# Experts' down products last, in two passes, with half of the second block's projections under the second pass

## The chip, the core and the metric

The kernel runs on one core of one Trainium2 chip. The metric is device microseconds of one execution, the median of several runs. All data are float32.

## What is computed

Two transformer blocks on x (256 tokens, 1024 features). The first ends in an expert-choice FFN with 16 experts of 32 tokens each and a hidden width of 2048; its result is normed. The second block projects its own norm of that by w_in_2 (7168 columns: q, k, v, z, two gates), adds a context, mixes, and ends in PEER, whose rows are gathered from a table. Cut to what matters here:

```python
hid = silu(einsum('becd,edf->becf', xs, w_gate)) * einsum('becd,edf->becf', xs, w_up)
eo = einsum('becf,efd->becd', hid, w_down)
x = x + zeros.at[bidx, idx].add(gates[..., None] * eo)       # first block, FFN
x = rms_norm(x, final_g)
h = modulate(rmsnorm(x, g_pre_mix), sh1, sc1)                # second block
q, k, v, z, gl = split_proj(h @ w_in_2)
y = mix_branches(rope(q), [kc, rope(k)], [vc, v], z, gl + b_gate, ...)
x_new = x + gt1 * rmsnorm(y, g_post_mix)
x = x_new + gt2 * rmsnorm(peer(modulate(rmsnorm(x_new, g_pre_ffn), sh2, sc2)), g_post_ffn)
```

## The kernel before, in words

Each engine has a program of its own, written as one Python function (`tensor`, `vector`, and so on); events are semaphore counts. A wait names an event, such as ("used", key) for "PE has finished with this weight block". PE is the matmul engine, DVE the vector engine, ACT the scalar engine, POOL the one that gathers, SP the one that issues the weight transfers. SP is one queue in program order: `load(slot, key, src)` waits for the last user of the slot in SBUF, then issues the transfer; `ring` takes the next slot of a list. A block is 2 MB (128 x 4096 floats).

Experts: for e in 0..15, `gate` and `upw` (four blocks each, L704) use 32 columns of the PE array per matmul, four column groups side by side; HID is transposed (L717); `down` (four blocks, L728) gives all 1024 features of the expert's 32 tokens in bank BE; DVE copies them (L1253), and four full-width matmuls (L742) with a gate matrix GE spread them over the tokens in banks YB. After expert 15, `block_out` and `gained` add and scale (L1266, L1270), `both_norms` and `norm_turn` make HT, the second block's input, features on partitions.

Second block: `mixer_order` returns ORDER, a list of stages that all engines walk. q, k and v (L800, `seven`) are made with seven instead of eight block products each, with DVE sums of weights (`wsum`) and inputs (`hsum`). `z`, `ga`, `gs` go through `tokens` (L416), eight matmuls of 128x512 each, one per half of the features and half of the tokens. They stand as fillers between the stages of the attention heads: `sc` scores (L837), `exp`, `cmb`, `trn` transpose (L846), `av` values (L858), `ao`. After the heads of token half a = 0 come `ba`, `op`, the norms and `ft`, then `qm` (L904), the first query product of PEER, then the gathers (`row`, L1994), which run to the end; the other half of the tokens is worked off beside them.

Of the kernel before, what the change touches and what calls it, by code (L numbers as in the profile page):

```python
# [14 lines left out]
NS = 6  # L15
SLOT = 4096
NARENA = 25832
# [104 lines left out]
def build(nc, D, out):  # L122
    from contextlib import ExitStack
    ctx = ExitStack()
    with ctx:
# [42 lines left out]
        LSUM, SSO, sub8, ssy, ss5, ss6, s8 = small(32), small(16), small(8), small(4), small(2), small(2), small(4)  # L168
        lamc = lam[:, 2:3]
# [14 lines left out]
        LATER, GE, OH, EO = ar(o, 8, 384), ar(o + 3072, 2, 2, 256), ar(o + 4096, 2, 512), ar(o + 5120, 2, 512)  # L184
# [4 lines left out]
        HDT = ar(o + 7168, 4, 128)  # L189
# [12 lines left out]
        YB, BG, BU, BH, BE = [0, 1, 2, 3], 4, 5, 6, 7  # L202

# [5 lines left out]
        RAW, RT, TMPG = ar(o + 14336, 2, 512), ar(o + 15360, 2, 512), ar(o + 14336, 2, 1024)  # L209
        PP, TT, AA, ATT = ar(o + 16384, 2, 2, 512), ar(o + 18432, 512), ar(o + 18944, 2, 512), ar(o + 19968, 2, 512)  # L210
        HSUM = ar(2048, 4, 4, 128)
        WSUM = {(m, i): ar(k, 4, 512) for m, at in (("k", (o + 8192, o + 12288, o + 6144)), ("q", (o + 16384, o + 18432, o + 10240)),
                                                    ("v", (o + 8192, o + 12288, o + 6144))) for i, k in zip((5, 6, 4), at)}
        DM, OYT = ar(o + 20992, 16, 8), HT
# [18 lines left out]
        def joined(m, a, n):  # L233
            d = QX[:, a, :, :].rearrange("p h t -> p (h t)") if m == "q" else VX[:, a, :]
            return d[:, n * 512:(n + 1) * 512]


        BLOCK = {"q": 0, "k": 2, "v": 4}
        RESULT = {1: (0, 0), 2: (0, 0), 6: (0, 1), 3: (0, 1), 4: (1, 0), 7: (1, 1)}
        place = [NARENA + i * SLOT for i in range(NS)] + [W0, SPARE, o + 21120, o + 14336, o, o + 16384, *PLACES]  # L240
# [7 lines left out]
        def mixer_order():  # L248
# [4 lines left out]
            def do(text):  # L253
                for word in text.split():
# [3 lines left out]
            do("norm_turn.0 seven.k.1 norm_turn.1 seven.k.2 hsum.0 wsum.k.5 hsum.1 wsum.k.6 seven.q.1 hsum.2 wsum.k.7 hsum.3 wsum.k.4 x3")  # L258
            do("seven.q.2 seven.k.5 seven.k.6 join.k.2 turned.k.0.0 join.q.2 wsum.q.5 wsum.q.6 seven.k.7 join.k.7 rope.k.0.0 seven.q.5 seven.k.4")
            do("turned.k.1.1 wsum.q.7 wsum.q.4 seven.k.3 join.k.3 turned.k.0.1 turned.k.1.0 seven.q.6 rope.k.1.1 seven.q.7 join.q.7")  # L260
            do("turned.q.0.0 turned.q.1.1 rope.k.0.1 seven.v.1 rope.k.1.0 seven.q.4 wsum.v.5 wsum.v.6 seven.q.3 join.q.3 turned.q.0.1")
            do("wsum.v.7 wsum.v.4 turned.q.1.0 seven.v.5 rope.q.0.0 rope.q.1.1 seven.v.6 seven.v.2 join.v.2 rope.q.0.1 seven.v.7 join.v.7")
            do("rope.q.1.0 seven.v.4 seven.v.3 join.v.3")
# [1988 lines left out]
```

## Time and profile before

| | |
|---|---|
| runs | 2100.95, 2101.39, 2102.20 us (median 2101.39) |
| profiled execution, span | 2100.0 us (what lies around it is not given; the median run is 1.4 us longer) |
| PE / DVE / ACT / POOL busy | 71% / 37% / 21% / 14% |
| bytes moved | 807.99 MB, mean 385 GB/s |
| chain that ended last | DMA 49%, PE 35%, DVE 9% |

The span is from the first to the last instruction of one execution. Busy shares are means over stages that differ; the stages have to be looked at one by one. In the profile each float32 matmul shows as two instructions, so a count such as x16 is eight matmuls of the program.

### The profile page before, as it was taken

How to read it: one execution, taken by the hardware profiler on the slowest of the kernel's cores; microseconds unless marked ns; L12 is line 12 of the kernel's file. 1: busy time of each engine (PE TensorE's matmuls, PEld its weight loads, DVE VectorE, ACT ScalarE, POOL GpSimd, SP SyncE). 2: the span in 40 equal slices, each digit the busy share in tenths (PEclk: the TensorE clock that was granted, in tenths of full speed). 3: DMA queues.
4: the chain of work that ended last, by engine and by line, in shares of the span. 5: the costliest groups of instructions: out<-in, count | busy, mean ns of one | idle time of the engine just before them, and what ended most of it. 6: DMA issues, size and time to landing. Idle time of an engine off the chain costs nothing.

```text
span 2100.0 us, 24929 instructions
## 1 busy us (share of the span) xinstructions
PE 1498.3 (71%) x10450; PEld 641.7 (31%) x10450; DVE 775.6 (37%) x1885; ACT 437.2 (21%) x990; POOL 302.6 (14%) x289
## 2 busy tenths in 40 slices
PE   9999756877676666566889999996667744444344
PEld 7654212332111111111344455553235510000001
DVE  5832101000000000000007443347667676867764
ACT  1331100000000000000002274453245622211212
POOL 0010000000000000000000000004334344544441
PEclk9999888898888778888999999997788865655555
DMA  9799999999999999999994556579999999999997
GB/s 401 288 402 424 427 427 428 427 428 428 428 427 428 428 428 427 428 428 428 427 410 191 211 196 240 209 290 387 405 422 418 420 421 420 421 421 420 421 421 293
DMA packets 76176, 807.99 MB, mean 385 GB/s; under 512 B 9024, under 2 KB 9152, under 8 KB 10400
## 3 DMA queue, kind: packets, MB, share of 16 engines
q1 hardware_dynamic: 38432, 537.74, 61.3%
q0 software_dynamic: 37632, 268.65, 30.9%
q8 instruction: 83, 1.36, 0.3%
q14 instruction: 29, 0.24, 0.0%
HBM read 805.11 MB, written 1.05 MB: 384 GB/s over the span
## 4 chain that ended last, share of the span: by engine, by line
DMA 49%; PE 35%; DVE 9%; ACT 3%; issue 2%; POOL 2%; DVEq 0%; ACTq 0%; POOLq 0%
DMA AR<-in_w_down 19%; DMA AR<-in_w_up 16%; DMA AR<-in_peer_uv,AR 15%; PE PS L416 11%; PE PS L427 4%; PE PS L800 3%; DVE AR L1580 3%; PE PS L704 3%; PE PS L728 2%; POOL AR L1994 2%; PE PS L947 2%; PE PS L537 1%; PE PS L904 1%; PE PS L742 1%; PE PS L494 1%
## 5 line engine op out<-in xcount | busy, mean ns | idle before, releaser
L1994 POOL DMA_INDIRECT AR<-in_peer_uv,AR x256 | 287.0, 1121 | 1611.9 <-DVE AR L1571 1307.2
L947 PE MATMUL PS<-AR 32*32 32x512 f32 x4032 | 219.6, 909 | 293.3 <-ACT AR L1932 293.2
L704 PE MATMUL PS<-AR 128*32 128x512 f32 x2048 | 297.9, 718 | 159.4 <-DMA AR<-in_w_up 111.6
L1580 DVE CUSTOM_DVE_ANT_0 AR<-AR 128x1024 f32<-128x1024 f32 x256 | 309.4, 1223 | 161.1 <-DMA AR<-in_peer_uv,AR 160.8
L416 PE MATMUL PS<-AR 128*128 128x512 f32 x544 | 243.3, 602 | 0.0
L728 PE MATMUL PS<-AR 128*32 128x512 f32 x1024 | 164.1, 775 | 88.4 <-DMA AR<-in_w_down 80.0
L1238 DVE TENSOR_TENSOR AR<-AR,PS 128x512 f32<-128x512 f32 x16 | 11.0, 688 | 581.3 <-PE PS L704 581.3
L704 PEld LDWEIGHTS PS<-AR 128*32 128x32 f32 x2048 | 62.2, 121 | 377.8 <-DMA AR<-in_w_up 179.3
L947 PEld LDWEIGHTS PS<-AR 32*32 32x32 f32 x4032 | 36.8, 125 | 431.9 <-ACT AR L1932 426.2
L416 PEld LDWEIGHTS PS<-AR 128*128 128x128 f32 x544 | 102.8, 193 | 127.1 <-issue 126.4
L1253 DVE COPY AR<-PS 128x512 f32<-128x512 f32 x16 | 11.1, 692 | 275.1 <-PE PS L728 275.1
L1926 ACT ACTIVATE AR<-AR 128x2 f32<-128x2 f32 x126 | 25.6, 203 | 380.0 <-DVE AR L1580 379.7
L1757 ACT ACTIVATE AR<-PS 128x512 f32<-128x512 f32 x16 | 9.6, 597 | 411.4 <-PE PS L704 411.4
L728 PEld LDWEIGHTS PS<-AR 128*32 128x32 f32 x1024 | 33.0, 127 | 199.1 <-DMA AR<-in_w_down 126.1
L427 PE MATMUL PS<-AR 128*128 128x256 f32 x384 | 84.2, 380 | 0.5 <-DVE AR L1013 0.5
L742 PE MATMUL PS<-AR 128*128 128x512 f32 x128 | 66.7, 669 | 14.5 <-DVE AR L1253 14.5
L427 PEld LDWEIGHTS PS<-AR 128*128 128x128 f32 x384 | 72.6, 190 | 14.0 <-issue 3.5
L800 PE MATMUL PS<-AR 128*128 128x512 f32 x168 | 74.3, 595 | 2.0 <-ACT AR L1821 1.2
L904 PE MATMUL PS<-AR 128*128 128x128 f32 x512 | 70.2, 302 | 7.1 <-DVE AR L1503 3.9
L904 PEld LDWEIGHTS PS<-AR 128*128 128x128 f32 x512 | 67.5, 216 | 13.2 <-issue 6.6
L1932 ACT ACTIVATE AR<-AR 128x32 f32<-128x32 f32 x252 | 67.3, 314 | 8.9
L437 PE MATMUL PS<-PK 128*128 128x256 f32 x248 | 62.8, 402 | 3.1 <-DMA PK<-in_pk 3.1
(297 smaller groups left out, 1389.9 us busy)
## 6 DMA issues: line engine op xcount, KB each, us to landing
AR<-in_w_up SPq DMA_DIRECT2D x64, 2048.0 KB, 25.7
AR<-in_w_down SPq DMA_DIRECT2D x64, 2048.0 KB, 26.4
AR<-in_w_gate SPq DMA_DIRECT2D x63, 2048.0 KB, 26.2
AR<-in_w_in SPq DMA_DIRECT2D x29, 2048.0 KB, 8.9
AR<-in_w_ada SPq DMA_DIRECT2D x12, 2048.0 KB, 13.7
AR<-in_w_out SPq DMA_DIRECT2D x6, 2048.0 KB, 8.2
AR<-in_peer_w_query SPq DMA_DIRECT2D x5, 2048.0 KB, 11.9
AR<-in_w_branch_sgu SPq DMA_DIRECT2D x4, 2048.0 KB, 7.6
```

The source lines that it names most:

```text
L416: i = pe.matmul(PS[:, b, :], src[:, j, a * 128:(a + 1) * 128], IN[key][:, j, :], start=(j == 0), stop=(j == 7))
L427: i = pe.matmul(PS[:, b, q * 256:(q + 1) * 256], IN[key][:, j, (e + q) * 128:(e + q + 1) * 128], src[:, j, :], start=(j == 0), stop=(j == 7))
L437: x = pe.matmul(PS[:, b, 0:256], ident, PK[:, 0:256], start=True, stop=True)
L704: x = pe.matmul(PS[32 * q:32 * q + 32, bk, :], XS[e][:, j, :], src[:, q * 512:(q + 1) * 512], start=(j == 0), stop=(j == 7), skip_group_ch ...
L728: x = pe.matmul(PS[32 * g:32 * g + 32, b, :], HDT[:, s, fq * 32:(fq + 1) * 32], IN[key][:, s, dc * 512:(dc + 1) * 512], start=(fq == 0 and ...
L742: x = pe.matmul(PS[:, y, :], GE[:, r, dc, a * 128:(a + 1) * 128], EO[:, r, :], start=(e == 0), stop=(e == 15), skip_group_check=True)
L800: y = pe.matmul(PS[:, b, :], a[:, j, :], x[:, j, :], start=(i in (1, 2, 5) and j == 0), stop=(i in (2, 3, 4) and j == 3), skip_group_check ...
L904: x = pe.matmul(PS[:, b, q * 128:(q + 1) * 128], IN[key][:, j, (2 * r + q) * 128:(2 * r + q + 1) * 128], HT[:, j, a * 128:(a + 1) * 128], ...
L947: x = pe.matmul(PS[c:c + 32, ACC[a][g], :], DI[t, p, r, :], AR[t, off + 1024 + m * 512:off + 1536 + m * 512], start=(h == 0 and p == 0), s ...
L1580: v.tensor_tensor_reduce(rows, rows, HB[:, a, :], 1.0, 0.0, MULT, ADD, DOT[:, ix, k:k + 1]).then_inc(*w.hit("dot", ix, k))
L1932: i = act.activation(DI[:, p, r, :], SG2[:, ix % 2, 2 * p + r, :], ACT.Copy, scale=two[:, r:r + 1])
L1994: pool.indirect_dma_start(out=AR[:, off:off + 2048], out_offset=None, in_=D["peer_uv_2"], in_offset=bass.IndirectOffsetOnAxis(ap=EI[:, ix, ...
```

## The change

1. The experts' loop computes only gate and up; all sixteen transposed HDT are kept. w_down follows in two passes (dc = 0, 1), each with 512 of the 1024 features, as 4 groups of four experts x 8 blocks of 2 MB (`down`). A block feeds eight matmuls on four column groups, one per expert. Two full-width matmuls per group of experts (`spread`) take the place of sixteen.
2. After the first pass features 0 to 511 of x are complete. They are scaled by final_g and g_pre, turned (`half_turn`), and multiplied with the first half of the rows of w_in_2 under the second pass (`ahead`: 14 half blocks "pre" of 1 MB, two token halves, four matmuls each). ACT copies each part to SBUF. The norm's factor and the shift are applied later; for the shift `ahead` sums shift times weights (four matmuls with 32 columns each, SHZ), and `bias_pairs` adds it up.
3. `rest` takes the place of `seven`, `z`, `ga` and `gs`: per projection pair and token half two bias matmuls over 32 rows and 2 x 4 matmuls over features 512 to 1023; DVE scales the early part and adds.
4. w_kv_2 holds the context's columns apart; context keys and values are spread over more experts. The order of stored features changes, so that no strided reads remain.

SP's part, with the places of the early halves:

```diff
+            ids[0], turn[0] = [2, 3, 4, 5, SA, SB], 0
+            w.wait_ge("mm", "vc", 1, 1)
+            for i in range(4):
+                for blk in range(8):
+                    if (i, blk) == (0, 5):
+                        w.wait_ge("mm", "upw", 15, 3)
...
+                    down(0, i, blk)
+            user[SA0] = user[SA1] = user[SA]
+            user[S50] = user[S51] = user[5]
+            ids[0], turn[0] = [2, 3, 4], 0
+            for i in range(4):
+                for blk in range(8):
+                    d = 8 * i + blk
+                    if d % 2 == 0 and d // 2 < len(AHEAD):
+                        early(d // 2, (SA0, SA1, S50, S51, SA0, SA1)[d // 2] if d < 12 else (S50, S51)[d // 2 % 2])
+                    down(1, i, blk)
```

PE's part:

```diff
+            def down(dc, i, blk):
...
+                for s2 in range(2):
+                    for g in range(4):
+                        x = pe.matmul(PS[32 * g:32 * g + 32, b, :], HDT[4 * q + g][:, 2 * sh + s2, fq * 32:(fq + 1) * 32], IN[key][:, g, s2, :],
+                                      start=(blk == 0 and s2 == 0), stop=(blk == 7 and s2 == 1), skip_group_check=True)
...
+            def ahead(m, n, a):
+                key = ("pre", m, n)
...
+                for j in range(4):
+                    x = pe.matmul(PS[:, b, :], HT[:, j, a * 128:(a + 1) * 128], IN[key][:, j, :], start=(j == 0), stop=(j == 3))
+                if a == 0:
...
+                    for j in range(4):
+                        g = 2 * n + j % 2
+                        pe.matmul(PS[32 * g:32 * g + 32, BB, :], SHZ[:, j, 31 - r:63 - r], IN[key][:, j, :], start=(m == AHEAD[0][0] and j < 2),
+                                  stop=(m == AHEAD[-1][0] and j > 1), skip_group_check=True)
+                x.then_inc(*w.hit("mm", "part", m, n, a, also=[("used", *key)] if a else ()))
...
+            for i in range(4):
+                for blk in range(8):
+                    down(1, i, blk)
+                    if i and blk == 0:
+                        spread(1, i - 1)
+                    if (i, blk) == (0, 1):
+                        half_turn(0)
+                        half_turn(1)
+                    elif (i, blk) > (0, 1) and todo:
+                        ahead(*todo.pop(0))
...
+            def rest(m, a):
...
+                for n in range(2):
+                    b, before = to[n]
+                    w.wait_ge(*before)
+                    p = slice(32 * (2 * n + a), 32 * (2 * n + a) + 32)
+                    pe.matmul(PS[:, b, :], same32[p, r:r + 1].broadcast_to([32, 128]), BIASB[p, :], start=True, stop=False)
...
+                for n in range(2):
+                    for j in range(4, 8):
+                        x = pe.matmul(PS[:, to[n][0], :], HT[:, j, a * 128:(a + 1) * 128], IN[key][:, n, j - 4, :], start=False, stop=(j == 7))
```

The fillers of the mixer:

```diff
-            first = [("z", 2, 0), ("z", 2, 1), ("z", 3, 0), ("z", 3, 1), ("zn1",), ("z", 0, 0), ("zn2",), ("z", 1, 0), ("zn3",), ("ga", 0, 0),
-                     ("zmix", 0), ("ga", 1, 0), ("zturn", 0), ("gs", 0, 0), ("gs", 1, 0), ("bs", 0, 0), ("bs", 1, 0)]
-            then = [("z", 0, 1), ("z", 1, 1), ("zmix", 1), ("ga", 0, 1), ("zturn", 1), ("ga", 1, 1), ("gs", 0, 1), ("gs", 1, 1), ("bs", 0, 1),
-                    ("bs", 1, 1)]
+            first = [("rest", "z2", 1), ("zn1",), ("rest", "z0", 0), ("zn2",), ("zn3",), ("rest", "ga", 0), ("zmix", 0), ("rest", "gs", 0),
+                     ("zturn", 0), ("bs", 0, 0), ("bs", 1, 0)]
+            then = [("rest", "z0", 1), ("zmix", 1), ("rest", "ga", 1), ("zturn", 1), ("rest", "gs", 1), ("bs", 0, 1), ("bs", 1, 1)]
```

How the rows of SP stand at the end of the experts, before the change (in_w_in stands for w_in and w_in_2; "waits s_mm" is a wait for a count of PE):

```order
L2017 DMA AR<-in_w_gate 128x4096 [waits s_mm] x4
L2017 DMA AR<-in_w_up 128x4096 [waits s_mm] x4
L2017 DMA AR<-in_w_down 128x4096 [waits s_mm] x4
L2017 DMA AR<-in_final_g 128x1024 [waits s_mm]
L2017 DMA AR<-in_w_in 128x4096 [waits s_mm] x2
```

and in the changed kernel, from early half 5 (the first row of in_w_in) to half 9 (the last one):

```order
L2098 DMA AR<-in_w_in 128x2048
L2098 DMA AR<-in_w_down 128x4096 [waits s_mm] x2
L2098 DMA AR<-in_w_in 128x2048
L2098 DMA AR<-in_w_down 128x4096 [waits s_mm] x2
L2098 DMA AR<-in_w_in 128x2048
L2098 DMA AR<-in_w_down 128x4096 [waits s_mm] x2
L2098 DMA AR<-in_w_in 128x2048 [waits s_mm]
L2098 DMA AR<-in_w_down 128x4096 x2
L2098 DMA AR<-in_w_in 128x2048 [waits s_mm]
L2098 DMA AR<-in_w_down 128x4096 x2
```

What moved: the down blocks wait for their own slots up to half 7; from half 8 on (six times in all) it is the half that waits, and the two down blocks behind it have no wait of their own.

PE's rows of a piece of the second pass in the changed kernel (L738 `down`, L772 `ahead`, L781 its bias sums, L751 `spread`):

```order
L738 MATMUL PS<-AR 32x512 x8
L772 MATMUL PS<-AR 128x512 x4
L738 MATMUL PS<-AR 32x512 x8
L751 MATMUL PS<-AR 128x512 x2
L772 MATMUL PS<-AR 128x512 x4
L781 MATMUL PS<-AR 32x512 x4
L738 MATMUL PS<-AR 32x512 x8
```

What moved: before, no projection stood among the down products; now each down block but four is followed by four full-width matmuls, and every second one by four bias sums too.

PE's rows in heads 5 to 8 of the mixer in the changed kernel (L887 scores, L896 transpose, L907 values, L413 `bs`, L854 and L860 `rest`):

```order
L413 MATMUL PS<-AR 128x512 x8
L896 MATMUL PS<-PK,AR 128x128 x4
L907 MATMUL PS<-AR 128x128 x4
L887 MATMUL PS<-AR 128x256 x4
L896 MATMUL PS<-PK,AR 128x128 x4
L907 MATMUL PS<-AR 128x128 x4
L887 MATMUL PS<-AR 128x256 x4
L896 MATMUL PS<-PK,AR 128x128 x4
L907 MATMUL PS<-AR 128x128 x4
L896 MATMUL PS<-PK,AR 128x128 x4
L907 MATMUL PS<-AR 128x128 x8
L887 MATMUL PS<-AR 128x256 x4
```

What moved: before, a group of eight L416 matmuls stood beside each of these heads; now several heads follow each other without one.

## Rows read from the trace of the kernel before

**Rows 1.** The page's slices: each digit is the busy share of 1/40 of the span

```profile
PE   9999756877676666566889999996667744444344
...
PEclk9999888898888778888999999997788865655555
DMA  9799999999999999999994556579999999999997
```

**Rows 2.** Stages: length, busy us of the engines (instructions), granted clock, DMA share, GB/s

```profile
600.00:800.00 200.00, 130.19 (x692) 29.61 (x696) 7.42 (x15) 4.13 (x7) 0.00 (x0) 0.75 1.01 428
...
1200.00:1250.00 50.00, 50.00 (x173) 25.23 (x172) 18.29 (x43) 34.41 (x62) 0.00 (x0) 1.00 0.45 168
...
1600.00:1800.00 200.00, 112.98 (x1547) 58.13 (x1556) 146.97 (x395) 82.27 (x190) 84.93 (x79) 0.70 1.01 421
```

**Rows 3.** Timeline of PE, down blocks: start, us, instruction, idle before and releaser

```profile
615.97 3.04 PE L728 MATMUL PS<-AR 128*32 128x512 f32 x16 [1.99 <-DMA AR<-in_w_down]
620.86 3.64 PE L728 MATMUL PS<-AR 128*32 128x512 f32 x16 [1.85 <-DMA AR<-in_w_down]
```

**Rows 4.** Timeline of PE at the experts' end

```profile
1041.83 3.67 PE L742 MATMUL PS<-AR 128*128 128x512 f32 x8 [0.90 <-DVE AR L1253]
1045.43 1.92 PE L704 MATMUL PS<-AR 128*32 128x512 f32 x16
1047.28 2.43 PE L437 MATMUL PS<-PK 128*128 128x256 f32 x10
1049.64 1.92 PE L704 MATMUL PS<-AR 128*32 128x512 f32 x16
...
1097.75 1.92 PE L728 MATMUL PS<-AR 128*32 128x512 f32 x16 [1.05 <-DMA AR<-in_w_down]
```

**Rows 5.** Timeline of PE: the first projection and the first query product

```profile
1110.90 3.67 PE L800 MATMUL PS<-AR 128*128 128x512 f32 x8 [0.82 <-ACT AR L1804]
...
1397.09 3.81 PE L904 MATMUL PS<-AR 128*128 128x128 f32 x32 [1.57 <-ACT PS L1883]
```

**Rows 6.** Timeline of POOL: the first gather

```profile
1412.82 1.01 POOL L1994 DMA_INDIRECT AR<-in_peer_uv,AR  x1 [1249.27 <-DVE AR L1571]
```

**Rows 7.** PE in the mixer: a group (count, busy, mean ns, idle), and timeline

```profile
L800 PE MATMUL PS<-AR 128*128 128x512 f32 x168 | 74.3, 595 | 2.0 <-ACT AR L1821 1.2 <-ACT AR L1804 0.8
...
1205.57 1.13 PE L837 MATMUL PS<-AR 64*128 64x256 f32 x8
1206.63 7.13 PE L416 MATMUL PS<-AR 128*128 128x512 f32 x16
1213.60 0.60 PE L846 MATMUL PS<-PK,AR 128*128 128x128 f32 x4
```

**Rows 8.** Timeline of ACT: one head, and the norm behind the first gs

```profile
1374.01 0.72 ACT L1869 ACTIVATE AR<-AR 128x512 f32<-128x512 f32 x1
1376.34 0.69 ACT L1861 ACTIVATE AR<-PS,AR 128x512 f32<-128x512 f32 x1 [1.61 <-DVE AR L1407]
...
1377.80 0.26 ACT L1881 COPY AR<-PS 128x128 f32<-128x128 f32 x1
...
1382.01 0.63 ACT L1854 ACTIVATE AR<-AR 128x512 f32<-128x512 f32 x1 [2.25 <-DVE AR L1392]
...
1385.70 1.06 ACT L1641 ACTIVATE AR<-AR 128x1024 f32<-128x1024 f32 x1 [1.55 <-DVE AR L1487]
```

**Rows 9.** The 12 issues of in_w_in, 2 MB each, between 1180 and 1400 us

```profile
DMA to landing us min/median/max: 7.4/7.5/9.0
```

**Rows 10.** Timeline of PE after a sparse stretch, and one window with its clock

```profile
1481.30 2.02 PE L947 MATMUL PS<-AR 32*32 32x512 f32 x32 [5.25 <-ACT AR L1932]
1483.26 8.99 PE L416 MATMUL PS<-AR 128*128 128x512 f32 x16
...
1494.46 7.13 PE L416 MATMUL PS<-AR 128*128 128x512 f32 x16
...
1480.00:1485.00 5.00, 3.70 (x34) 1.13 (x35) 4.76 (x14) 2.29 (x6) 0.96 (x2) 0.50 1.01 423
```

More of the change, by code:

```diff
@@ L16 @@
 SLOT = 4096
-NARENA = 25832
+NARENA = 25904
 PACK = [
@@ L498, in ada_columns @@
             def ada_columns():
-                _, before = banks.use("mod", 5, at=BE)
-                w.wait_ge(*before)
+                for h in range(2):
+                    _, before = banks.use("mod", h, at=(BE, YB[0])[h])
+                    w.wait_ge(*before)
                 w.wait_ge("pkb")
@@ new lines, in spread @@
+            def spread(dc, i):
+                q = QUADS[dc][i]
+                w.wait_ge("geq", q)
+                w.wait_ge("eo", dc, q)
+                for a in range(2):
+                    y = YB[2 * dc + a]
+                    if i == 0:
+                        _, before = banks.use("x2", dc, a, at=y)
+                        w.wait_ge(*before)
+                    x = pe.matmul(PS[:, y, :], GEQ[:, q, a * 128:(a + 1) * 128], EO[:, i % 2, :], start=(i == 0), stop=(i == 3),
+                                  skip_group_check=True)
+                    if i == 3 and a == 0:
+                        x.then_inc(*w.hit("mm", "y", dc, a))
+                x.then_inc(*w.hit("mm", "spread", dc, q, also=[("mm", "y", dc, 1)] * (i == 3)))
@@ new lines, in bias_pairs @@
+            def bias_pairs():
+                b, before = banks.use("bias4")
+                w.wait_ge(*before)
+                w.wait_ge("bsum")
+                w.wait_ge("pairsum")
+                pe.matmul(PS[:, b, :], PAIRSUM, BIASB, start=True, stop=True).then_inc(*w.hit("mm", "bias4"))
+            for i in range(4):
+                for blk in range(8):
+                    down(0, i, blk)
+                    if i and blk == 0:
+                        spread(0, i - 1)
+            spread(0, 3)
@@ L755, in tensor @@
+            assert not todo
+            spread(1, 3)
             keep_busy("norm", n=8, at=BG)
             banks.ids = list(range(8))
-            h2m = [[("turned", "h3", a, 0), ("moved", "h3", a, 1)] for a in range(2)]
+            h2m = [[("turned", "h3", a), ("moved", "h3", a)] for a in range(2)]
             def norm_turn(a):
-                turn("scaled", "h3", XN[:, a, :], True, a, ("xn4", a), second="moved")
+                for tag, j0 in (("turned", 4), ("moved", 6)):
+                    b, before = banks.use(tag, "h3", a)
+                    w.wait_ge(*before)
+                    w.wait_ge("xn4", a)
+                    for j in (j0, j0 + 1):
+                        x = pe.transpose(PS[:, b, (j - j0) * 128:(j - j0 + 1) * 128], XN[:, a, j * 128:(j + 1) * 128], ident)
+                    x.then_inc(*w.hit("mm", tag, "h3", a))
@@ L764, in rope @@
             def rope(x, n, a):
-                b, before = banks.use("kq", x, n, a, at=3 + a)
+                b, before = banks.use("kq", x, n, a)
                 w.wait_ge(*before)
@@ new lines, in vector, with gathered @@
+            for q in range(4):
+                w.wait_ge("igq", 3)
+                v.tensor_scalar(GEQ[:, q, :], pk("iota_t"), IGQ[:, 0, q:q + 1], IGQ[:, 1, q:q + 1], EQ, MULT).then_inc(*w.hit("geq", q))
+            w.wait_ge("shz0")
+            v.tensor_copy(SHZ[:, :, 31:32], COL[:, 5, 0:4].unsqueeze(2)).then_inc(*w.hit("shz"))
+            def gathered(dc, i):
+                q = QUADS[dc][i]
+                w.wait_ge("mm", "eo", dc, q)
+                if dc or i > 1:
+                    w.wait_ge("mm", "spread", *((dc, QUADS[dc][i - 2]) if i > 1 else (0, QUADS[0][2 + i])))
+                v.tensor_copy(EO[:, i % 2, :], PS[:, BH + i % 2, :]).then_inc(*w.hit("eo", dc, q))
@@ L1794, in scalar @@
+            for a in range(2):
+                squares(0, a)
+                gained_squares(0, a)
+            for m, n in AHEAD:
+                for a in range(2):
+                    w.wait_ge("mm", "part", m, n, a)
+                    act.copy(part_of(m, a, n), PS[:, banks.at("part", m, n, a), :]).then_inc(*w.hit("part", m, n, a))
             act.activation(s8[:, 2:3], ident[:, 0:1], ACT.Sqrt)
             for a in range(2):
-                w.wait_ge("x2", a, 1)
-                act.activation(Y[:, a, :], X[:, a, :], ACT.Square, scale=1.0 / 32, accum_out=ss3[:, a:a + 1]).then_inc(*w.hit("sumsq", "x3", a))
+                squares(1, a)
```

560 lines of the change are left out of this document (281 added, 279 removed).

## The prediction

> **What bounds the kernel now.** I read the page's slices first [rows 1]: for most of the first half the 16 DMA engines are full (about 428 GB/s) while TensorE (PE) is partly idle; then the DMA falls to about half and PE is full; then the DMA is full again to the end. The stages put numbers on it [rows 2]: 600 to 800 us has a DMA share of 1.01 with PE busy 130.19 of 200 us, 1200 to 1250 us has PE busy 50.00 of 50 us at a DMA share of 0.45, and 1600 to 1800 us has a share of 1.01 again. So the experts are bound by their weights, the second block's mixer by PE, the last part (gathered rows) by DMA. The timeline of PE shows the cadence of the experts: down blocks of 2 MB start 4.90 us apart, each ended by the DMA [rows 3]. The experts' last down block starts on PE at 1097.75 us [rows 4]; the first projection at 1110.90, and the first query product, which ends the mixer's first half, at 1397.09 [rows 5]. The gathers begin 15.7 us later [rows 6]. What comes behind the query product isn't changed in kind, so I price the change by the time at which that product starts.
>
> **The mixer gets shorter.** PE between 1110.90 and 1397.09 (286.2 us) holds 84 matmuls of the seven-product scheme and 128 of z, ga and gs (each shows as two instructions). A 128x512 matmul costs 0.871 us, from 16 instructions that push the next start back by 6.97 us [rows 7]: 212 x 0.871 = 184.7 us leave. There come 112 of the same size (97.6 us) and 28 bias matmuls over 32 rows, in pairs on different row groups and banks. Nearest row: four 256-column matmuls on two row groups take 1.07 us [rows 7], so a pair of 512 columns takes 1.0 (0.87 if perfectly side by side, 1.74 if not): 13 us for the 13 pairs that aren't hidden, bounds 11 and 23. PE's work is then 286.2 - 184.7 + 97.6 + 13 = 212 us, and 1 less for h3's fewer transposes.
> But its cover is gone. Before, nearly each attention head stood beside a 7 us filler; now heads 6 and 7, the tail of both halves, and head 9 have none. A head without filler takes the chain ACT copy, DVE combine, DVE maximum, ACT exponentials: from 1374.01 to 1377.80 [rows 8], and 1.3 us of ACT copies and squares after it, about 5.1 us against 2.5 us of PE. Two full heads and two draining steps give 8 us, head 9 with its turn 2.5. Behind the last gs the chain sigmoid, root, sum, square took 4.75 us (1382.01 to 1386.76) [rows 8] and now has 5 us of PE beside it where it had 12; with the copies and the second root I get 6.5. Together 17 us (between 5 and 30). Mixer: 211 + 17 = 228 us, 58 less. The removed wsum and hsum work of DVE cost nothing (PE had only 2 us of stalls at L800) [rows 7]. The second halves' twice as large ACT work lies under the next filler.
>
> **What the experts pay.** 14 half blocks of 1 MB, final_g and b_gate are loaded ahead of the last down block; at 2 MB in 4.90 us that alone is 34.3 + 1.8 us. The first pass ends at 1097.75 - 32 x 4.90 + 1.8 = 942.8. PE has 1.85 us of work per block there, so it stays bound by DMA. In the second pass the part matmuls begin with the third down block: 3 blocks and 2 halves later, at 962.4.
> From here a pair of down blocks with one early half costs PE: 2 x 1.85 (eight 32-column matmuls, 1045.43 to the next start at 1047.28) [rows 4], 8 x 0.871 = 6.97, four bias sums (32 columns of the array each, on two column groups), and changes between narrow and full tiles. The sums' price isn't in the trace: 0.9 if they ran four abreast as L704 does, 3.5 one by one; I take 1.74, two by two, since the code alternates two groups. A change costs 0.12 (four L742 matmuls push the next start back by 3.60, not 3.48) [rows 4]; three make 0.34. Pair: 12.75 us, over the DMA's 12.25: PE binds.
> The Trainium skill (TensorEngine Tiling (Array Packing), Key Properties) says changing the tiling mode drains the engine, which speaks against mixing such tiles. Its rule gives no time. The highest price that the rows allow is 0.18 a change (five 256-column L437 matmuls push the next start back by 2.36, not 2.18 [rows 4]); at four changes a pair would be 0.38 dearer and the end 5 us later. The trace agrees with the rule only as far as this small price.
> The 14 new half blocks save nothing else in this stage: the 48 fewer spread matmuls (L742) lay under DMA.
>
> **The wait that it adds.** The early halves 0 to 5 have four places, but from half 6 on only two, S50 and S51. Half i then waits for half i-2, whose last use is the matmul behind down block 2i-1. SP (one queue) issues half i, then down blocks 2i and 2i+1. So for i = 8 to 13 SP may issue neither the half nor the next down block before PE has finished everything it had. The order shows this: six rows of in_w_in with a wait, and behind each two of in_w_down without one; their own slots are long free. Six times PE and DMA both empty. The empty time: a 2 MB block takes 7.5 us from issue to landing on a quiet queue [rows 9]; a 1 MB half ahead of it adds 2.45, the semaphore 0.15: 10.1 us. Bounds: 7.5 (the block overtakes the half) and 12.4 (the two down blocks share the engines).
> After such a gap the clock is low: PE had been idle for 5.25 us before 1481.30, the granted clock was 0.50, the 1.2 GHz level, at 1480 to 1485 us, and eight matmuls took 8.99 us, against 7.13 at 1494.46, in dense work, at the 2.4 GHz level [rows 10]. These lose 1.9; with the narrow matmuls ahead of them I take 2.5 us a gap (0 to 6). The Trainium skill (TensorE: Matmul & The Clock Gate, What's actually happening) puts the ramp at under 1% of a typical span and warns against fitting it. Going by it without the ramp, the end would be 15 us earlier, which is part of rival B. The stretch of [rows 10] shows a ramp, so I keep it.
> Timeline: 962.4 + 7 pairs x 12.75 + one spread 1.75 + 2 of ramp = 1055.4. Six cycles of 10.1 + 12.75 + 2.5 = 25.35, and two spreads: 155.6, so 1211.0. Last pair 12.75, two blocks 3.7, bias 0.9: 1228.3, where before the last block ended at 1099.6: **128.7 us later**. From there to the first projection 11.3 us before [rows 4, 5]; half the width of copy, add, square and scale, and one matmul less, save 3.7. So the first projection starts at 1235.9, 125.0 later, and the query product at 1464, 66.8 later. All later work has the same instructions and the same order of release of the row places, so the end moves as much: 2100.0 + 66.8 = 2166.8. The median of the runs lies 1.4 above the profiled span: **2168 us**.
>
> **Rivals.**
> A, the gaps fill: the six waits open before PE runs dry. Then 6 x 12.6 us fall away (10.1 of gap, 2.5 of ramp): 2168 - 76 = 2092 us, **faster** by 9. What decides is the loss per cycle: above 1.5 us (8.8 / 6) the sum is slower than before. For it: the first seven pairs do run so. Against it: the order's rows; a filled gap would need a down block in flight that has not been issued. Chance 4%.
> B, smaller gaps: landing after 7.5 us, no ramp, narrow sums partly under the down blocks: 6 x 5.1 + 12 = 43 less, 2125 to 2145. For it: the ramp and the sums are priced from far rows. Chance 15%.
> C, dearer pairs: the two-column sums go one by one (14 x 1.75 = 24 us), the clock stays at 1.2 GHz through a cycle (6 x up to 6 = 36 us): 2195 to 2230. For it: in the experts' stage sparse work ran at 0.50 for whole groups. Against: dense work brought 1.00 back within a group [rows 10]. Chance 14%.
> D, off-setting losses: gaps of 3 us only and a mixer without stalls would land within 0.2% of before (4.2 us, about what a measurement of this kernel can tell). Chance 2%.
>
> **How the numbers follow.** The forecast has 65%: 2168, 2145 to 2195 by its bounds (gap 15, stalls 12, ramp 15, bias 10, not all on one side). The range takes most of B and a part of C: 2133 to 2200. Faster has A's 4%, same 2%, slower the rest, 94%.
>
> **What will show it.** In the profile of the changed kernel: DMA share near 1 to about 1050 us, then six dips of DMA and PE together, 25 us apart, until about 1210; SP's in_w_in and the two in_w_down issued within a microsecond there; PE ended by DMA of w_down with about 10 us idle each; first L860 near 1236 and first L953 near 1464, so 228 us for the mixer with some 17 us of idle, most of it released by ACT. I am wrong if w_down blocks are in flight across these six points, or if the mixer doesn't shrink by 40 to 70 us.

## The result, and the profile after

The changed kernel takes **2219.11 us** (median; 2217.74 to 2222.53), the kernel before 2101.17 on the same chip: ratio 1.056, 95% interval 1.055 to 1.058. It is slower, as forecast, but by 118 us, not by 67; 2219 lies above the range. The profiled span is 2215.9 us, 115.9 more than before, and that is what the steps below add up to.

The page's slices, as in [rows 1]:

```profile
PE   9998676776565655659855988897686854434445
...
PEclk9999888877777777889977999898686975565555
DMA  9699989999999999999455824357999999999997
```

The dip of DMA at 4-5-5 (about 1050 to 1220 us) was forecast. The low second digit stands in the kernel before too (7 there); the 8 at the sixth digit (277 to 332 us) was not forecast. Windows put numbers on it (columns as in [rows 2]), first of the kernel before:

```profile
180.00:240.00 60.00, 50.84 (x356) 22.06 (x348) 5.75 (x14) 3.33 (x7) 0.00 (x0) 0.94 1.00 425
300.00:480.00 180.00, 131.18 (x744) 52.53 (x744) 10.73 (x19) 5.78 (x10) 0.00 (x0) 0.85 1.01 427
```

and of the changed one:

```profile
180.00:240.00 60.00, 46.51 (x332) 18.23 (x324) 8.06 (x36) 9.64 (x15) 0.00 (x0) 0.92 0.92 381
300.00:480.00 180.00, 132.73 (x672) 56.92 (x672) 3.37 (x5) 9.90 (x17) 0.00 (x0) 0.87 0.89 375
480.00:960.00 480.00, 284.84 (x1608) 57.51 (x1604) 9.72 (x17) 10.05 (x17) 0.31 (x1) 0.77 1.01 428
```

At a full share of 1.01, a share of 0.92 over 60 us and of 0.89 over 180 us lose 5.3 and 21.4 us of loading, 27 us in all. The experts are bound by their weights, so this should come out as lateness later. The timeline of PE holds the milestones that answer to [rows 4, 5]:

```profile
969.20 1.92 PE L738 MATMUL PS<-AR 128*32 128x512 f32 x16 [1.46 <-DMA AR<-in_w_down]
...
992.30 3.70 PE L772 MATMUL PS<-AR 128*128 128x512 f32 x8
...
1090.85 3.59 PE L738 MATMUL PS<-AR 128*32 128x512 f32 x16 [9.90 <-DMA AR<-in_w_down]
...
1116.93 3.64 PE L738 MATMUL PS<-AR 128*32 128x512 f32 x16 [9.96 <-DMA AR<-in_w_down]
...
1246.57 1.92 PE L738 MATMUL PS<-AR 128*32 128x512 f32 x16
...
1257.03 7.13 PE L860 MATMUL PS<-AR 128*128 128x512 f32 x16
...
1514.35 3.81 PE L953 MATMUL PS<-AR 128*128 128x128 f32 x32 [0.80 <-ACT AR L1892]
```

In order: the last block of pass 1, the first early product (a product of `ahead`, L772), two of the six gaps, the last down block, the first projection, the first query product. From there to the end of the span it is 701.6 us, and was 702.9: nothing behind the query product changed. SP's rows at the gaps:

```profile
1080.98 0.33 SPq L2098 DMA_DIRECT2D AR<-in_w_in  x1
1081.35 0.91 SPq L2098 DMA_DIRECT2D AR<-in_w_down  x2
1107.01 0.33 SPq L2098 DMA_DIRECT2D AR<-in_w_in  x1
1107.38 0.91 SPq L2098 DMA_DIRECT2D AR<-in_w_down  x2
```

The half and its two down blocks are issued together, within about a microsecond, when PE has run dry (its last early product before the gap ends at 1080.95), and the down block is there 9.9 us later. PE's waits in the mixer (us in total, times, longest):

```profile
PE PS L896 <- DVE AR L1479: 12.5, 4, 6.3
PE PS L838 <- DVE AR L1423: 10.1, 4, 2.5
PE PS L413 <- ACT AR L1704: 4.0, 1, 4.0
PE PS L413 <- DVE AR L1062: 2.0, 1, 2.0
```

and its largest group there:

```profile
L860 PE MATMUL PS<-AR 128*128 128x512 f32 x224 | 106.4, 630 | 0.1
```

The group L860 should have taken 112 x 0.871 = 97.6 us by my working. What stretches it is seen at one of the four waits of L838, the transposes of a rotated half of q or k:

```profile
1297.40 0.63 PE L838 MATMUL PS<-PK,AR 128*128 128x128 f32 x4 [2.53 <-DVE AR L1423]
1297.95 1.13 PE L854 MATMUL PS<-AR,PK 32*128 32x512 f32 x4
1299.01 8.83 PE L860 MATMUL PS<-AR 128*128 128x512 f32 x16
```

and a window over the start of the last row:

```profile
1299.00:1304.00 5.00, 5.00 (x10) 2.26 (x9) 1.69 (x5) 0.00 (x0) 0.00 (x0) 0.66 0.00 0
```

After a wait of 2.53 us, eight matmuls take 8.83 us instead of 7.13, and the window over their first 5 us has a mean granted clock of 0.66: about two thirds of it at the 1.2 GHz level, although PE was busy for the whole window.

So there are three places: the gaps (expected), holes in the DMA during experts 1 to 7, and short waits with a slow clock behind them in the mixer. The experiments take them one at a time. All are edits of the changed kernel unless said otherwise, so their medians are compared with 2219.1. The kernel before, run again beside each of them, took 2100.2 to 2101.1 us.

### The profile page after: what moved, and what is told of

Same layout as the page of the kernel before. It is cut to its first block, busy times and chain, and to the rows that moved or that the text cites. A ratio compares the mean times of both kernels' runs of the same rounds, so it can differ in the third digit from the quotient of the medians.

```text
span 2215.9 us, 24722 instructions
## 1 busy us (share of the span) xinstructions
PE 1514.1 (68%) x10356; PEld 613.8 (28%) x10356; DVE 742.5 (34%) x1862; ACT 429.9 (19%) x998; POOL 309.4 (14%) x290
## 3 DMA queue, kind: packets, MB, share of 16 engines
q0 software_dynamic: 37632, 268.65, 29.3%
## 4 chain that ended last, share of the span: by engine, by line
DMA 42%; PE 42%; DVE 9%; ACT 3%; issue 2%; POOL 0%; SPq 0%; DVEq 0%; another core or an unknown queue 0%; ACTq 0%; POOLq 0%
DMA AR<-in_peer_uv,AR 13%; DMA AR<-in_w_up 12%; DMA AR<-in_w_down 10%; PE PS L413 5%; DMA AR<-in_w_gate 5%; PE PS L699 5%; PE PS L860 5%; PE PS L772 5%; PE PS L424 4%; PE PS L738 4%; DVE AR L1638 3%; PE PS L996 3%; PE PS L953 2%; PE PS L535 1%; PE PS L781 1%
## 5 line engine op out<-in xcount | busy, mean ns | idle before, releaser
L699 PE MATMUL PS<-AR 128*32 128x512 f32 x2048 | 330.1, 782 | 202.9 <-DMA AR<-in_w_up 129.3
L2072 POOL DMA_INDIRECT AR<-in_peer_uv,AR x256 | 293.6, 1147 | 1071.8 <-DVE AR L1629 772.7
L996 PE MATMUL PS<-AR 32*32 32x512 f32 x4032 | 224.7, 907 | 288.5 <-ACT AR L2008 285.2
L738 PE MATMUL PS<-AR 128*32 128x512 f32 x1024 | 177.9, 756 | 131.4 <-DMA AR<-in_w_down 130.8
L413 PE MATMUL PS<-AR 128*128 128x512 f32 x288 | 136.1, 629 | 7.3 <-ACT AR L1704 4.0
L1320 DVE COPY AR<-PS 128x512 f32<-128x512 f32 x8 | 5.5, 692 | 315.8 <-PE PS L738 315.8
L860 PE MATMUL PS<-AR 128*128 128x512 f32 x224 | 106.4, 630 | 0.1
L772 PE MATMUL PS<-AR 128*128 128x512 f32 x224 | 104.2, 608 | 0.0
L738 PEld LDWEIGHTS PS<-AR 128*32 128x32 f32 x1024 | 34.8, 125 | 246.8 <-DMA AR<-in_w_down 174.0
L413 PEld LDWEIGHTS PS<-AR 128*128 128x128 f32 x288 | 56.6, 201 | 81.9 <-issue 79.9
L424 PEld LDWEIGHTS PS<-AR 128*128 128x128 f32 x384 | 73.5, 193 | 17.5 <-issue 5.1
L953 PEld LDWEIGHTS PS<-AR 128*128 128x128 f32 x512 | 67.5, 216 | 11.3 <-issue 5.9
L1882 ACT COPY AR<-PS 128x512 f32<-128x512 f32 x28 | 16.4, 586 | 250.9 <-PE PS L772 250.9
## 6 DMA issues: line engine op xcount, KB each, us to landing
AR<-in_w_gate SPq DMA_DIRECT2D x63, 2048.0 KB, 21.1
```

The costliest lines, as they stand in the source:

```text
L413: i = pe.matmul(PS[:, b, :], src[:, j, a * 128:(a + 1) * 128], IN[key][:, j, :], start=(j == 0), stop=(j == 7))
L424: i = pe.matmul(PS[:, b, q * 256:(q + 1) * 256], IN[key][:, j, (e + q) * 128:(e + q + 1) * 128], src[:, j, :], start=(j == 0), stop=(j == 7))
L699: x = pe.matmul(PS[32 * q:32 * q + 32, bk, :], XS[e][:, j, :], src[:, q * 512:(q + 1) * 512], start=(j == 0), stop=(j == 7), skip_group_ch ...
L738: x = pe.matmul(PS[32 * g:32 * g + 32, b, :], HDT[4 * q + g][:, 2 * sh + s2, fq * 32:(fq + 1) * 32], IN[key][:, g, s2, :], start=(blk == 0 ...
L772: x = pe.matmul(PS[:, b, :], HT[:, j, a * 128:(a + 1) * 128], IN[key][:, j, :], start=(j == 0), stop=(j == 3))
L860: x = pe.matmul(PS[:, to[n][0], :], HT[:, j, a * 128:(a + 1) * 128], IN[key][:, n, j - 4, :], start=False, stop=(j == 7))
```

## Experiments

**e1: the early halves behind their down blocks.**

```diff
-                    if d % 2 == 0 and d // 2 < len(AHEAD):
+                    if d % 2 == 0 and d < 16:
                         early(d // 2, ...)
                     down(1, i, blk)
+                    if d % 2 == 1 and 16 < d < 28:
+                        early(d // 2, (S50, S51)[d // 2 % 2])
```

> Edit: the early halves 8 to 13 of w_in_2 are issued behind their two down blocks in SP's order, not ahead of them; nothing else moves. My theory (a half waits for its slot, and the two down blocks queued behind it on SP arrive late): the six PE gaps of 9.9 to 10.0 us ahead of a down block (L738, ended by in_w_down) go, with the short clock loss behind each, so 6 x (9.95 + about 2) = about -72 us against the changed kernel's 2219, that is about 2147; the last down block ends near 1177 us and not 1248.5. Rival (the second pass is limited by the DMA's bytes: two down blocks and a half per 24.5 us are as much as the queues bring): the gaps stay in sum, only in front of another matmul, and the time stays within 10 us of 2219.

2150.4 us (2141.6 to 2151.3), 68.7 less. The six waits for w_down are gone, but for one of 0.37 us. Timeline of SP:

```profile
1078.82 0.33 SPq L2098 DMA_DIRECT2D AR<-in_w_in  x1
1079.19 1.84 SPq L2098 DMA_DIRECT2D AR<-in_w_down  x2
1093.21 0.33 SPq L2098 DMA_DIRECT2D AR<-in_w_in  x1
```

a window of the second pass:

```profile
1050.00:1100.00 50.00, 50.00 (x216) 16.91 (x217) 0.69 (x1) 4.69 (x8) 0.00 (x0) 1.00 0.86 347
```

and the first projection, 72.4 us earlier than in the changed kernel's profile (the profiled execution of e1 is its fastest, 2141.6 us; its first early product already starts 2.5 us earlier, at 989.80, where nothing was changed, so 69.9 us are left for the second pass):

```profile
1184.68 7.13 PE L860 MATMUL PS<-AR 128*128 128x512 f32 x16
```

The half still waits for PE as before, but the down blocks that PE needs next are in flight already. PE is busy for 50.00 of 50 us at full clock, and the DMA has room (0.86). The rival, that the DMA's bytes bind the second pass, falls. In the changed kernel the six gaps add up to 59.7 us, and the clock behind them cost 1.3 to 2.3 us each, 10.7 together, by the starts of its down blocks: 70.4 us, close to what e1 gave.

**e2: context products in one piece.**

```diff
-                        if (name, c) == ("gate", 1):
-                            if e in (4, 5):
-                                context_keys(e - 4, 2)
-                            elif e in (6, 7):
-                                context_values(e - 6, 1)
...
                     context_keys(e - 3, 0)
+                    context_keys(e - 3, 2)
...
                     context_values(e - 5, 0)
+                    context_values(e - 5, 1)
```

> Edit: the context key and value products are each done in one piece at the end of an expert, not half of it behind the next expert's second gate piece, so that the ring slot of the context weight comes free an expert piece earlier. Theory H (slot holding): the first early product (L772), which starts at 992.3 us in the changed kernel and which I had put at 964, comes about 15 to 25 us earlier, the DMA share of 300 to 480 us returns to 0.95 to 1.0, and the time is about 2219 - 20 = 2199. Rival R (the ring of four, then five slots is too short by itself for experts 1 to 7, where the kernel before had six): the start of L772 moves by under 5 us and the time stays at 2214 to 2219. A third, which would make it slower: the whole product at the end of an expert keeps PE from the next expert's gate, +5 us.

2205.9 us (2198.8 to 2208.3), 13.2 less. The first early product starts at 978.14 (14.2 earlier), and the window from 300 to 480 us has recovered two thirds:

```profile
300.00:480.00 180.00, 137.58 (x716) 58.81 (x712) 3.37 (x5) 9.89 (x17) 0.00 (x0) 0.87 0.97 407
```

What the split does can be read from SP. In the changed kernel, with expert 5's gate and up blocks on either side of the pause:

```profile
337.17 16.41 SPq L2098 DMA_DIRECT2D AR<-in_w_gate  x4
375.79 2.21 SPq L2098 DMA_DIRECT2D AR<-in_w_up  x4
```

and in e2:

```profile
333.55 17.68 SPq L2093 DMA_DIRECT2D AR<-in_w_gate  x4
369.00 5.64 SPq L2093 DMA_DIRECT2D AR<-in_w_up  x4
```

With the product cut in two, the w_kv block keeps its slot until PE has done two gate blocks of the next expert. SP, one queue in order, stands behind that slot for 22 us (353.6 to 375.8) and issues the four up blocks at once when the second half of the key product ends on PE (375.7). Undivided, the pause is 18 us. So holding a slot costs, but about half of the 27 us stays: neither expectation was right by itself.

**e3: ropes of one token half not back to back.** Both halves of the features of a token half a pass through one buffer, RT[:, a], and ORDER had them next to each other.

```diff
-... turned.k.0.0 turned.k.1.0 rest.q.0 rope.k.0.0 rope.k.1.0 turned.k.0.1 turned.k.1.1
-rest.v.0 rope.k.0.1 rope.k.1.1 turned.q.0.0 turned.q.1.0 rest.v.1 rope.q.0.0 rope.q.1.0 rest.q.1 turned.q.0.1 turned.q.1.1
-rest.z2.0 rope.q.0.1 rope.q.1.1
+... turned.k.0.0 turned.k.0.1 rest.q.0 rope.k.0.0 rope.k.0.1 turned.k.1.0 turned.k.1.1
+rest.v.0 rope.k.1.0 rope.k.1.1 turned.q.0.0 rest.v.1 rope.q.0.0 turned.q.1.0 rest.q.1 rope.q.1.0 turned.q.0.1
+rest.z2.0 rope.q.0.1 turned.q.1.1
...
-            first = [("rest", "z2", 1), ("zn1",), ...
+            first = [("rest", "z2", 1), ("rope", "q", 1, 1), ("zn1",), ...
```

> Edit: in the written order the two halves n=0 and n=1 of one token group a are no longer turned back to back through the one buffer RT[:, a]; the other token group's comes between. Theory (DVE can write the second turned half only when PE has transposed the first, and the short stalls of 2.5 us let the clock fall): the four L838 waits of 2.53 us (10.1 us) go, and three of the four L860 groups at 8.8 us that follow return to 7.1 us (5 to 7 us), so about -15 to -17 us: 2202 to 2204. Rival (the waits are DVE's own work on the rope, which is the same in any order): they move to other transposes and the time stays within 4 us of 2219.

2197.5 us (2195.6 to 2198.4), 21.6 less, some 5 more than expected. The L838 waits are gone and L860 is back near its price:

```profile
L860 PE MATMUL PS<-AR 128*128 128x512 f32 x224 | 99.9, 599 | 0.1
```

That is 10.1 us of waits and 6.5 in this group; the bias matmuls (L854) went from 16.9 to 15.8. The rival falls: DVE's work is the same, only its place isn't.

**e4: the wait kept, but filled.** Six filling matmuls stand in front of each rope of the second feature half.

```diff
             def rope(x, n, a):
+                if n:
+                    keep_busy("rope", x, a, n=6)
```

> Edit: six filling matmuls are put in front of each n=1 rope, so that PE waits as long as before but is busy while it does. If the price of a stall is the stall and the clock that falls behind it: the L860 groups behind the stalls are 7.1 us and not 8.8 us, the wait itself stays (partly as filling matmuls, 6 x about 0.22 to 0.43 us), total about -5 to -7 us: 2212 to 2214. Rival (the clock behind the stalls falls for another reason, such as a throttle of the whole stretch): the groups stay at 8.8 us and the time is 2219 or 1 to 4 us more.

2211.0 us (2209.5 to 2212.0), 8.1 less: more work, and a faster kernel. The wait turned into fillers, and the group behind it takes 7.13:

```profile
1296.61 2.76 PE L434 MATMUL PS<-PK 128*128 128x256 f32 x12
1299.31 0.63 PE L840 MATMUL PS<-PK,AR 128*128 128x128 f32 x4
1299.86 1.13 PE L856 MATMUL PS<-AR,PK 32*128 32x512 f32 x4
1300.92 7.13 PE L862 MATMUL PS<-AR 128*128 128x512 f32 x16
```

A window over such a group, which answers to the one with 0.66:

```profile
1289.00:1294.00 5.00, 5.00 (x13) 2.20 (x12) 1.94 (x5) 0.00 (x0) 0.00 (x0) 1.00 0.00 0
```

So of e3's 21.6 us about 8 are the clock and 10.1 the waits. The 3 or so that are left I can't place; between the two profiled executions the difference is 19.3 us (2215.9 to 2196.6), which leaves about 1. The rival (a throttle of the whole stretch) falls.

**e5 and e6: one slot more for experts 1 to 6.** Slot 1 is idle in the changed kernel until HDT[6] is written over it. With it the ring has five slots in experts 1 to 3 (four in the changed kernel) and six from expert 4's up blocks to expert 6 (five in the changed kernel). e6 is e5 with e2's undivided context products.

```diff
-            turn[0], ids[0] = 0, [2, 3, 4, 5]
+            turn[0], ids[0] = 0, [2, 3, 4, 5, 1]
...
-                            turn[0], ids[0] = 4, [*ids[0][turn[0] % 4:], *ids[0][:turn[0] % 4], P6]
+                            turn[0], ids[0] = 5, [*ids[0][turn[0] % 5:], *ids[0][:turn[0] % 5], P6]
...
                 elif e in (5, 6):
+                    if e == 6:
+                        at = turn[0] % 6
+                        ids[0] = [k for k in [*ids[0][at:], *ids[0][:at]] if k != 1]
+                        turn[0] = 0
```

> Edit: slot 1, which lies idle in experts 1 to 6, joins the ring of weight loads for them (five slots from expert 1, six with P6 from expert 4 until expert 6's products are issued, then five as now); the context products stay in two pieces. The whole products of e2 gave 13.2 us and brought L772 from 992.3 to 978.1; windows of DMA share still lose about 5 us at 180 to 240 us and 7 us at 300 to 480 us. Theory H2 (the ring's depth is the cause, and holding a slot for longer costs only because the ring is short): L772 comes 20 to 27 us earlier, at 965 to 972, and the time is 2219 - 20 to 27 = 2192 to 2199. Rival (the depth does not matter, the split does): only the 5 us of 180 to 240 go, 2212 to 2216.

> Edit: e5's six slots and e2's undivided context products together. H2: with enough slots the split costs nothing more, so this is within 3 us of e5, at 2192 to 2199, with L772 at 965 to 968 where my forecast put it (964.3). Rival (two separate causes): e5 and e2 add up, 13 us below e5.

e5: 2198.0 us (2197.7 to 2199.0), 21.1 less; e6: 2194.6 us (2194.2 to 2195.4), 24.5 less. In e5 the products are still cut in two, and yet the first early product comes 20 us earlier,

```profile
972.00 3.70 PE L772 MATMUL PS<-AR 128*128 128x512 f32 x8
```

and the window is nearly full:

```profile
300.00:480.00 180.00, 133.80 (x726) 55.70 (x728) 2.75 (x4) 10.16 (x18) 0.00 (x0) 0.90 0.99 421
```

Here the undivided products add 3.4 us; alone (e2) they gave 13.2. The two are not separate causes: the ring is too short, and in a short ring it matters how long a slot is held. In e6 the first early product starts at 969.08, 4.8 behind my 964.3; 180 to 240 us still loses (share 0.93).

**e11: the same from the other side.** The kernel before, with its ring cut from six slots to four for experts 1 to 3 and five for experts 4 to 6, and six again from expert 7 on (the changed kernel stays at five).

```diff
             for e in range(16):
+                if e in (1, 4, 7):
...
+                    old = ids[0][turn[0] % len(ids[0]):] + ids[0][:turn[0] % len(ids[0])]
+                    if e == 1:
+                        ids[0] = [k for k in old if k not in (0, 1)]
+                    else:
+                        ids[0] = old + [{4: 0, 7: 1}[e]]
+                    turn[0] = len(ids[0]) - 1 if e > 1 else 0
```

> Edit, on the kernel before: its ring of six slots is cut to what the changed kernel has, four for experts 1 to 3 and five for experts 4 to 6, six again from 7; nothing else. H2 (a ring this short cannot cover the stretches in which PE does the context's products and the later slots' selection, and every hole of the DMA is paid in full because loads bound the experts): 5 to 20 us slower than before, 2105 to 2120, with the DMA share of 180 to 480 us under 1.00. Rival (the short ring only hurts where the context products are cut in two, or where no down blocks are in the stream): within 3 us of 2100.

2111.8 us (2109.6 to 2112.1) against 2100.7: ratio 1.005 (1.003 to 1.006), 11 us slower, without anything of the change in it.

```profile
180.00:240.00 60.00, 45.82 (x321) 16.58 (x320) 3.96 (x10) 2.25 (x4) 0.00 (x0) 0.92 0.87 365
300.00:480.00 180.00, 127.09 (x756) 54.23 (x748) 12.57 (x22) 6.84 (x12) 0.00 (x0) 0.90 1.00 423
```

Most is lost with four slots (180 to 240 us: 0.87), hardly any with five. In the changed kernel the ring has four slots until 323 us, where SP issues expert 4's up blocks:

```profile
300.00:323.00 23.00, 22.32 (x116) 16.13 (x116) 1.30 (x2) 1.64 (x3) 0.00 (x0) 0.95 0.62 261
323.00:480.00 157.00, 110.41 (x561) 40.79 (x564) 2.06 (x3) 8.25 (x14) 0.00 (x0) 0.86 0.94 392
```

By these shares it loses 5.3 + 8.9 = 14 us with four slots and 11 with five, where the shortened kernel before loses hardly any. The likely reason is that its experts load 8 blocks each, not 12, and that its context products are cut in two; no run separates these. A ring of five is enough where no context product stands: 480 to 960 us of the changed kernel has a share of 1.01. So the depth matters at the places where PE does other work between two experts.

**e7: `zturn` earlier, on top of e3.**

```diff
                     if todo[-1][0] in ("rest", "bs"):
+                        if fill and fill[0] == ("zturn", 0):
+                            todo.append(fill.pop(0))
                         return
```

> Edit, on top of e3: in the written order zturn.0 stands right behind rest.gs.0 instead of right ahead of bs.0.0, so that PE has six short groups between the transposes and the product that needs ACT's copies. Theory (the 3.96 us in front of L413, ended by ACT L1704, is the copy's latency, and the slow 8.8 to 9.95 us group behind it is the clock): 4.0 us of stall and 1.7 to 2.8 us of clock go, so e3's 2197.5 less about 6: 2191 to 2192. Rival (ACT, in its own order, makes something else late instead, the softmax of the next head): the stall moves to an L896, and the time stays at 2196 to 2198.

2192.0 us (2190.0 to 2197.2), 5.4 below e3 by the medians (the slowest of the four lies within e3's range). The wait of 3.96 us ahead of L413 (L415 here) is gone and the group has its 7.13:

```profile
1360.59 7.13 PE L415 MATMUL PS<-AR 128*128 128x512 f32 x16
```

The softmax did not become later: the waits for it are 13.0 us in all, as in e3.

**e8: e1, e2, e3, e5 and e7 together.**

> Edit: e1, e2, e3, the six slots of e5 and the early zturn of e7 in one kernel. If the three misses are separate places on one path of PE, the gains add: 68.7 (e1) + 21.6 (e3) + about 23 (ring, with e2) + about 6 (e7) = 119, so 2219 - 119 = about 2100, level with the kernel before (2101). Rival (they share cover: with the path shorter, the DMA's 428 GB/s or a load that had been early enough is late in the second pass or in the mixer): 2110 to 2130, with a DMA releaser in front of L738 or L860. If it comes out under 2097, the two-pass scheme itself gains over the kernel before.

2099.3 us (2094.5 to 2102.4) against 2100.2: ratio 0.9993 (0.998 to 1.000). The gains add: 119 expected, 119.8 measured, where e1, e3, e6 and e7 by themselves give 68.7 + 21.6 + 24.5 + 5.4 = 120.2. The milestones, pass 2's start, the first projection and the query product:

```profile
970.20 4.91 PE L771 MATMUL PS<-AR 128*128 128x512 f32 x8
...
1165.51 7.13 PE L859 MATMUL PS<-AR 128*128 128x512 f32 x16
...
1396.30 3.81 PE L952 MATMUL PS<-AR 128*128 128x128 f32 x32 [0.80 <-ACT AR L1889]
```

The mixer takes 230.8 us, with 16 us of waits in it. The query product starts 0.8 us ahead of [rows 5]. So the two-pass scheme itself is neither gain nor loss here, once these places are mended: the 54.6 us by which the first projection comes later are what the mixer saves (286.2 - 230.8 = 55.4).

**e9 and e10: fillers moved, on top of e8 and of e9.**

```diff
-                filler(first)
+                if s not in (5, 7):
+                    filler(first)
```

> Edit, on top of e8: the fillers skip heads 5 and 7 in the first ten, so that the last two (bs.0.0 and bs.1.0, 7.1 us each) lie in heads 6 and 8, where PE waits 1.18, 2.15 and 3.37 us for DVE L1478 one head after the other. Theory (each wait is the softmax latency of a head that has nothing beside it): two of the three waits go, and heads 5 and 7, now without a filler, get waits of 1 to 2 us of their own: -2 to -4 us against e8's 2099.3, so 2095 to 2097. Rival (the latency per head is the same wherever the filler stands): 2098 to 2100.

```diff
-            steps([("up1", 0), ("up2", 0)], pairs[8], [("fn1", 0), ...
+            steps([("up1", 0), ("up2", 0)], pairs[8])
+            filler(then)
+            steps([("fn1", 0), ...
...
                      ("qse", 1, 0)]
-            filler(then)
             filler(then)
```

> Edit, on top of e9: the product bs.0.1 is moved from behind the query scores (where two of them, 13.9 us, lie side by side) to between up2.0 and fn1.0, in front of the 6.26 us that PE waits for DVE L1478. Theory: that wait goes and what is left behind the query scores, 7 us of cover, is still enough for the selection's DVE chain: -4 to -6 us against e9, so 2090 to 2093. Rival (the selection chain was covered by both products): the wait reappears in front of L995 (ended by ACT L2005), 2094 to 2100.

e9: 2095.5 us (2093.1 to 2100.4), ratio to the kernel before 0.998 (0.997 to 0.999), a gain of about 5 us. The mixer went from 230.8 to 227.7 us, but the four waits of L896 only from 13.0 to 11.9; the other 2 us are PE's busy time, and most of them are the clock. The stretch from head 7's transpose to the next projection, first in e8 and then in e9:

```profile
1299.16:1305.23 6.07, 6.07 (x32) 4.58 (x32) 0.52 (x3) 3.75 (x10) 0.00 (x0) 0.72 0.01 3
1297.35:1301.86 4.51, 4.51 (x33) 3.26 (x33) 0.17 (x1) 3.18 (x9) 0.00 (x0) 1.00 0.02 4
```

The same work takes 1.56 us less at full clock. In e8 two waits, of 2.15 and 3.37 us, stand close before it, in e9 one of 3.30. e10: 2095.0 us (2091.3 to 2096.7), no further. There the rival holds: the 6.3 us in front of L896 went, and came back behind the scores. Timeline of PE behind the query scores, in e9:

```profile
1421.61 1.52 PE L996 MATMUL PS<-AR 32*32 32x512 f32 x32 [3.48 <-ACT AR L2006]
```

and in e10:

```profile
1420.56 2.02 PE L997 MATMUL PS<-AR 32*32 32x512 f32 x32 [7.79 <-ACT AR L2007]
```

## Why the prediction was right or wrong

| step | forecast | measured |
|---|---|---|
| last block of pass 1 starts (the prediction calls it the end) | 942.8 us | 969.2 |
| first early product | 964.3 | 992.3 |
| pair of down blocks with a half | 12.75 | 12.67 |
| gap (PE's idle time) | 10.1 | 9.90 to 10.00 |
| clock loss per gap | 2.5 | 1.3 to 2.3, mean 1.8 (from one gap's down block to the next, less the gap, 12.67 for the pair and 1.82 where there is a spread; the most: 1116.93 to 1141.84 is 24.91, less 9.94 and 12.67) |
| last down block's end to first projection | 7.6 | 8.5 |
| mixer | 228 | 257.3 |
| query product to the end of the span | 702.9 | 701.6 |

**Right: the wait that it adds.** Six gaps of about 10 us, caused by the order on SP. e1 removed them by moving nothing but that order and got back 68.7 us, against the 76 that rival A allowed for them. Of the gap's terms no run shows the 0.15 for the semaphore by itself; the first of the two blocks starts on PE 9.50 us after its issue (1081.35 to 1090.85). The pair's price, the bias sums (two by two: one row pair L781 + L738 shows 1.7 us above a block's own 1.85) and the shorter chain to the first projection held. From the first early product to the first projection I had 271.6 us; it took 264.7, and 4.3 of the 6.9 between them are the clock behind the gaps, which I had too dear.

**Wrong, first: "The first pass ends at 1097.75 - 32 x 4.90 + 1.8".** This took [rows 3]'s cadence as given for the whole first half, back to expert 1. I priced the blocks that move, and not the ring that carries them: the change takes two of six slots away during experts 1 to 3 and one from expert 4 on (HDT lies over slot 0, and from expert 6 on over slot 1), and holds one longer through the divided context product. That put holes of 27 us into a DMA that had none, and the first early product came 28 us late. e5 and e6 gave back 21 and 24.5 us, e11 cost the kernel before 11.

**Wrong, second: the mixer's term "Together 17 us" of waits.** The places that I named (head 9 and the heads without filler, the chain behind the last gs) came to 12.5 us: 6.3 for the heads where I had 10.5, and 6.3 for the chain where I had 6.5. Three places that I had not looked at added 16.1: the ropes (10.1), `zturn` (4.0), the turn of the heads `ht` (2.0). With 0.8 in front of the query product the waits are 29.4 us. The 10.1 could be read in ORDER at the mixer's start: two ropes of one token half one behind the other, through one buffer, 2.53 us of DVE between them. Before, seven-product matmuls stood between them, and I checked only the fillers of the heads.

**Wrong, third: the clock in the mixer at nothing.** I charged the ramp only behind 10 us gaps. e4 shows about 8 us of it behind four waits of 2.53 us. Behind the waits of `zturn` and `ht` the group takes 8.80 instead of 7.13 us, and the small matmuls near the other waits are slower too. So the 29 us by which the mixer is dearer than forecast are 12.4 of waits (29.4 against 17) and about 17 of PE's own time (257.3 - 29.4 = 227.9 against 211). In e8, with the ropes' and `zturn`'s waits gone, that time is 215.0, so 13 of the 17 are clock behind waits that could be removed; the rest is in the main the clock behind those that stayed, by the starts in the timeline. The Trainium skill (TensorE: Matmul & The Clock Gate, What's actually happening) puts the ramp at under 1% of a typical span. Here the 10.7 us behind the gaps and an estimated 16 in the mixer are 27 us, 1.2% of the span, in these two stretches alone; the measurement decides. It is a small share of the span, but against a change that is worth tens of microseconds it has to be priced.

The sum: 21.1 us at the first projection (28.0 late at the start, 6.9 less in pass 2 and behind it), 29.3 in the mixer, 1.3 less behind it: 2166.8 + 21.1 + 29.3 - 1.3 = 2215.9, the span. Rival C had the right size for a wrong reason: it wanted the sums one by one and a clock that stays low in pass 2, and neither is so. The first two misses are of one kind: something that the change takes from stages it does not seem to touch.

## What to carry to other kernels

When a change makes data live longer in SBUF, price the buffers that it takes from the transfer ring, and how long each slot is held, before pricing the work: a DMA-bound stage pays every hole in full. On an in-order transfer queue, issue what is needed next ahead of what has to wait for a slot; here that order alone was worth 69 us. And when work is taken out, read the new order for pairs that share one buffer and now stand back to back: the short waits cost their length and, behind them, most of that again in slow matmuls (8 us on 10), so that here harmless work in their place made the faster kernel.

## What the runs showed of the hardware

- A wait of PE of 2.53 us can be enough to lower the clock. The next eight 128x512 matmuls took 8.60 to 8.83 us in the changed kernel and up to 9.66 in e1, and 7.13 with six filling matmuls in the wait's place (e4). It doesn't follow every such wait: in e1 the group behind one of the four waits of L838 (2.54 us, at 1226.74) took 7.13, and in e8 the group behind the 2.02 us ahead of L415 took 7.11, where in the changed kernel the same wait (2.03 us) was followed by 8.80.
- The slow part comes after the wait, in dense work. The window that holds the wait (1281 to 1286 us) had a granted clock of 0.94, the next one, with PE busy throughout, 0.72.
- Alternating 32-column and 128-column tiles cost next to nothing here: 12.67 us a pair (two down blocks with one early half), where the matmuls alone make 12.41 (2 x 1.85, 8 x 0.871, and 1.74 for the sums, of which the trace shows 1.70), with PE busy 50.00 of 50 us at full clock and a DMA share of 0.86 (e1).
